# A third copy of the expert program: the second block of 32 tokens outside the loop

## What is computed

```python
def run_block(args):
    tok, e = args
    xb = xf[tok]
    hid = jax.nn.silu(xb @ w_gate[e]) * (xb @ w_up[e])
    return hid @ w_down[e]
...
y = jnp.zeros((n_tok, d), f32).at[buf_t].add(outs.reshape(cap, d).astype(f32) * buf_w[:, None])
```

## Time and profile before

| | us |
|---|---|
| median of 3 runs | 1020.96 |
| lowest and highest of them | 1017.95, 1021.09 |
| the profiled execution, its own time | 1017.99 |
| its span in the trace | 1016.3 |
| PE busy in the span | 813.8 |
| PEld busy | 658.0 |
| VectorE busy | 491.5 |
| ScalarE busy | 362.5 |
| GpSimd busy | 49.7 |
| read from HBM | 277.13 MB |

### The profile page before, as it was taken

How to read it: one execution, slowest core, us unless ns; L and a number is a source line. 1 busy time by engine, 2 the same in 40 slices (tenths; PEclk the granted TensorE clock), 3 DMA queues, 4 the chain that set the end, 5 groups by cost and what they waited for, 6 DMA issues and landing times.

```text
span 1016.3 us, 21184 instructions
## 1 busy us (share of the span) xinstructions
PE 813.8 (80%) x8057; PEld 658.0 (65%) x8058; DVE 491.5 (48%) x791; ACT 362.5 (36%) x505; POOL 49.7 (5%) x143
## 2 busy tenths in 40 slices
PE   5999789799999998879998787686655655767563
PEld 5999579699999998868988564353322332333231
DVE  3554788667878746555893633232312211232222
ACT  5432585364645544444873421111101011010102
POOL 4000100000000000110040000000000000000000
PEclk9999999799999999889999899898889887998887
DMA  7586222269898755053423956799999999999993
GB/s 262 185 285 232 84 83 84 92 257 352 292 314 292 262 200 170 17 166 115 133 85 127 425 221 249 309 423 429 427 425 425 429 425 424 428 427 426 425 429 137
DMA packets 88256, 278.71 MB, mean 274 GB/s; under 512 B 7279, under 2 KB 67098, under 8 KB 70810
## 3 DMA queue, kind: packets, MB, share of 16 engines
q1 hardware_dynamic: 87518, 276.84, 70.5%
q10 hardware_dynamic: 700, 1.36, 0.4%
HBM read 277.13 MB, written 1.05 MB: 274 GB/s over the span
## 4 chain that ended last, share of the span: by engine, by line
PE 58%; DMA 21%; DVE 9%; issue 5%; ACT 5%; PEld 1%; POOL 1%; SPq 0%; PEldq 0%; POOLq 0%; DVEq 0%; ACTq 0%
DMA Whi<-in_w_up 20%; PE bank L1785 10%; PE bank L380 9%; PE bank L381 9%; PE bank L382 9%; PE bank L1806 3%; PE acc L431 2%; PE bank L1515 1%; PE acc L1520 1%; PE acc L1515 1%; PE bank L1518 1%; PE acc L1518 1%; PE bank L1520 1%; DVE rms L437 1%; PE bank L1797 1%
## 5 line engine op out<-in xcount | busy, mean ns | idle before, releaser
L380 PE MATMUL bank<-R_r,Whi_r 128*128 128x256 f32 x800 | 233.3, 292 | 18.6 <-DVE R_r L2065 7.2
L381 PE MATMUL bank<-R_r,Whi_r 128*128 128x256 f32 x800 | 230.5, 288 | 0.0
L382 PE MATMUL bank<-R_r,Whi_r 128*128 128x256 f32 x720 | 207.1, 288 | 0.0
L380 PEld LDWEIGHTS bank<-R_r,Whi_r 128*128 128x128 f32 x800 | 157.6, 197 | 24.0 <-issue 18.3
L381 PEld LDWEIGHTS bank<-R_r,Whi_r 128*128 128x128 f32 x800 | 157.8, 197 | 0.1
L382 PEld LDWEIGHTS bank<-R_r,Whi_r 128*128 128x128 f32 x720 | 141.7, 197 | 0.0
L2518 DVE TENSOR_TENSOR V<-V,bank 64x256 f32<-64x256 f32 x34 | 14.4, 424 | 244.2 <-ACT V L1282 244.2
L1785 PE MATMUL bank<-Whi,S 128*32 128x256 f32 x832 | 65.0, 481 | 43.8 <-DMA Whi<-in_w_up 29.0
L1282 ACT ACTIVATE V<-bank 64x256 f32<-64x256 f32 x34 | 12.8, 376 | 213.7 <-PE bank L1785 213.7
L311 ACT ACTIVATE Whi_r<-Wlo 128x1024 fp32r<-128x1024 f32 x64 | 63.9, 1049 | 66.7 <-PE bank L382 66.3
L2010 DVE TENSOR_TENSOR Whi_r<-Wlo,Whi_r 128x2048 fp32r<-128x2048 f32 x33 | 75.6, 2289 | 25.0 <-ACT Whi_r L1083 12.2
(11 more groups left out here) (490 smaller groups left out, 1583.6 us busy)
## 6 DMA issues: line engine op xcount, KB each, us to landing
Wlo<-in_w_in SPq DMA_DIRECT2D x24, 1024.0 KB, 5.3
Wlo<-in_w_gate_up SPq DMA_DIRECT2D x22, 1024.0 KB, 5.1
Whi<-in_w_gate SPq DMA_DIRECT2D x10, 2048.0 KB, 26.0
Whi<-in_w_up SPq DMA_DIRECT2D x10, 2048.0 KB, 30.4
Whi<-in_w_down SPq DMA_DIRECT2D x10, 2048.0 KB, 32.2
projR<-in_w_up SPq DMA_DIRECT2D x9, 2048.0 KB, 37.0
Wlo<-in_w_gate SPq DMA_DIRECT2D x9, 2048.0 KB, 27.1
Wlo<-in_w_up SPq DMA_DIRECT2D x9, 2048.0 KB, 31.5
```

The source lines that it names most:

```text
L380: pe.matmul(o, w_hi[:, c], tile(x_hi, k), start=(k == 0), stop=False)
L381: pe.matmul(o, w_hi[:, c], tile(x_lo, k), start=False, stop=False)
L382: mm = pe.matmul(o, w_lo[:, c], tile(x_hi, k), start=False, stop=(k == KT - 1))
```

## The change

On GpSimd, ScalarE, TensorE and VectorE alike, the second window of an expert gets straight code of its own behind `If(windows > 1)`. The inner loop runs over w = 2 to 7, and stands behind a second test, `If(windows > 2)`. Each par holds three copies of the window program, nine in all. No operation, wait, transfer or buffer changes.

```diff
@@ gpsimd
                     gather(0)
                     with pool.If(windows > 1):
-                        with pool.Fori(1, NWIN) as w:
-                            with pool.If(windows > w):
-                                gather(w)
+                        gather(1)
+                        with pool.If(windows > 2):
+                            with pool.Fori(2, NWIN) as w:
+                                with pool.If(windows > w):
+                                    gather(w)
@@ scalar
                     window(before + 1)
                     with act.If(windows > 1):
-                        with act.Fori(1, NWIN) as w:
-                            with act.If(windows > w):
-                                window(before + w + 1)
+                        window(before + 2)
+                        with act.If(windows > 2):
+                            with act.Fori(2, NWIN) as w:
+                                with act.If(windows > w):
+                                    window(before + w + 1)
@@ tensor
                     window(None, before + 1)
                     with pe.If(windows > 1):
-                        with pe.Fori(1, NWIN) as w:
-                            with pe.If(windows > w):
-                                window(w, before + w + 1)
+                        window(1, before + 2)
+                        with pe.If(windows > 2):
+                            with pe.Fori(2, NWIN) as w:
+                                with pe.If(windows > w):
+                                    window(w, before + w + 1)
@@ vector
                     window(0, before + 1)
                     with dve.If(windows > 1):
-                        with dve.Fori(1, NWIN) as w:
-                            with dve.If(windows > w):
-                                window(w, before + w + 1)
+                        window(1, before + 2)
+                        with dve.If(windows > 2):
+                            with dve.Fori(2, NWIN) as w:
+                                with dve.If(windows > w):
+                                    window(w, before + w + 1)
```

## The result

The changed kernel is slower: 1184.37 us (median of 4; 1178.05 to 1185.3) against 1020.21 us (median of 4; 1017.95 to 1021.09), a ratio of 1.160 with a 95% interval of 1.1555 to 1.1645, or +164 us. The forecast was 1019.9 us, the range 1016 to 1046; of its cases the strong form of "code that no longer stays" came true, and above its own price.

The account below looks back on a forecast made before the run. The prediction took the weight stream as the bound, so of TensorE's 26 us only the filled dip counted: -1.15 + 0.1 for more code = -1.05 us, from 1020.96 to 1019.9 us, range 1016 to 1046.

Parts of the forecast that it names:

- strong form: Rival, 0.17: on TensorE each hop misses its code, a round takes 51 us, +66 us, about 1086 us.
- code that no longer stays: Rival, slower, 0.50: TensorE's loop body grows from 5.5 to 8.3 packets, no longer fits on chip, each round fetches again.
- What bounds the kernel: In the expert rounds the weight stream at about 427 GB/s is the bound, 14.7 us per expert, not an engine.
- Steps 1 and 2: TensorE after ranks 1, 5, 18 and 20: empty passes gone, 17.7 us; faster clock for the next experts, 8.4 us.
- Step 3: Second windows on TensorE gain 0; the weight stream's dip at 656 to 664 us is filled, -1.15 us.
- Step 4: Three more window copies in TensorE's program, 2.8 instruction packets to fetch: bounds 0 and +2.9 us, +0.1 taken.
- mild form: Rival, 0.33: only a round's last and first code on TensorE displace each other; +11.1 us, 1031 us.
- The hop's price: TensorE's jump over a copy to code not kept: 4.8 us under load, an estimated 2 us at idle.
- The hole: Rival, 0.05: weight stream's standstill at 636 to 640 us closes if rank 0's exit shortens; -4.4 us more, 1015.5 us.
- The exit: In the mild form, TensorE behind the last expert: three more jumps at 2 us, 1.3 us free, +4.7 us.

Follow-up runs that it names:

- e7: Changed kernel without the inner loop of buffers 1 and 2 on all four engines, seven copies: 1015.96 us, ratio 0.9981 against the kernel before.
- e5: Kernel before, plus a never-run third window copy in TensorE's program for buffer 0 only, seven copies: 1017.86 us.
- e6: Kernel before, plus never-run third window copies in TensorE's program for buffers 0 and 1, eight copies: 1111.81 us.
- e10: Changed kernel with every weight transfer from rank 3 on cut to an eighth, instructions and waits the same: 1075.62 us.
- e4: Kernel before, two copies kept, inner loop ending at the expert's own number of windows on all four engines: 1013.01 us, ratio 0.9956.
- e3: Kernel before, plus a never-run third window copy per buffer in TensorE's program, inside the outer loop: 1198.32 us.
- e9: Kernel before, plus 22 never-run combines (352 matmuls) in TensorE's program between the outer loop and the end: 1020.44 us.

## Why the prediction was wrong, step by step

- **What bounds the kernel: right.** The stream bound before, and where TensorE's 26 us were freed without growing past the store (e7) they brought 1.9 us (0.4 to 3.6).
- **Steps 1 and 2, gaps and clock: right in e7, undone in the changed kernel.** TensorE in order of time of the changed kernel, its ranks 1 and 2:

```profile
626.17 5.16 PE L1789 MATMUL bank<-Wlo,S 128*32 128x256 f32 x64 [4.69 <-issue]
...
643.28 0.63 PE L1789 MATMUL bank<-w_gate,S 128*32 128x256 f32 x4 [0.84 <-issue]
...
647.69 0.64 PE L1789 MATMUL bank<-projR,S 128*32 128x256 f32 x2 [3.79 <-issue]
```

  The gap after rank 1 is 0.84 us instead of 5.39, as forecast (0.67); but four matmuls later TensorE stands for 3.79 us, at what I read as the first packet not yet fetched. Rank 5's load is issued at 654.22, not at 647.4: from 654.88 before, nothing is won.
- **Step 3, second windows and the dip: right in e7**, -1.9 us measured for -1.05.
- **Step 4, more code: the step that failed.** I bounded it from what a packet costs once (0 to 2.9 us, +0.1 taken), that is, as if each extra packet were fetched one time. The question was how often. The runs show some ten packets in every round, 86 behind 664 us, and +164 us, where the sum had +0.1. The trace of before shows that 5.5 packets and headers stay, and the changed loop has 8.3 and headers. "As likely as not" was fair for the store's size, and the rival named the mechanism; but I gave the forecast 0.45 and the strong form 0.17, and ended the range at 1046, ahead of the strong form's own time. Seven copies fit and eight don't, by e5 and e6: the changed kernel, with nine, was two past the step. The Trainium skill, "Runtime: NRT & Kernel Launch", section "Instruction fetch mechanics", gives TensorE eight blocks of 16 KiB; read as a size of what a loop may hold, e5 and e6 agree to within a packet: 7 x 0.92 = 6.4 packets and headers stay, 7.4 and headers don't. By size alone eight copies could still fit into eight blocks; they don't only if the packet ahead, or a block that the body fills in part, counts too, and no run splits that. I had cited it as neither shown nor refuted, and should have let it shift the chances.
- **The mild form (0.33): wrong.** It let only the round's last and first code displace each other. The rows show ten packets in each round and a gap ahead of every expert.
- **The strong form: right in mechanism, 98 us short in size (1086 for 1184).** Three terms were small. The gaps of a round were put at 22 us and measure 30.5: the crossing inside the third expert (2.46 us) was not counted, and the round's end takes 14.73 us instead of 11.0. The windows were put at 29.1 us and take 61.15 - 30.5 = 30.65. So a round is 17 us over the stream, not 7, and eight rounds make 8 x 17 = 136 us. The third is the pace of before: its eight rounds, from rank 3's load at 618.40 to rank 27's at 955.78 us, took 337.4 us and not 8 x 44.1 = 352.8, which is 15.4 us more. In the changed kernel the same loads lie at 617.87 and 1115.44 us, 497.6 us apart, 8.4 us over 8 x 61.15: the round with rank 18's second window takes 68.80 us. Those with the second windows of ranks 5 and 20, at a round's end, take only 61.92 and 61.77, since the gap behind such a window is 8.60 and 8.48 us instead of 14 to 15. With 7.5 us behind the last of these loads that is 136 + 15.4 + 8.4 + 7.5 = 167 us, the difference of the two spans.
- **The hop's price (4.8 us under load, 2 us idle): a microsecond low.** In the rounds shown the gaps between experts are 6.47 and 6.81 us, and 3.62 and 3.97 us with a light stream; 0.67 of each is there anyway, so a hop is 5.8 to 6.1 and 3.0 to 3.3 us. The round's end was the expensive one. The sequencer's row for the loop's closing branch in the changed kernel (ns), and in e10:

```profile
L1826 PEldq COMPARE_BRANCH  x1: 7407/7407/7407, 847.4 to 847.4; - x1
```

```profile
L1829 PEldq COMPARE_BRANCH  x1: 4737/4737/4737, 750.0 to 750.0; - x1
```

- **The hole (0.05): wrong for this change, right as a mechanism.** It stayed open, since rank 0's exit kept its gap (4.69 us). e4 closed it and gained 4.5 us, where the rival said 5.5.
- **The exit: near.** The rival put its three jumps, less what is free, at +4.7 us; the gap ahead of the last combine grew by 3.8. In the changed kernel the gap ahead of the last expert is 8.76 us, and ahead of the last combine 6.05, where 2.23 stood:

```profile
1159.01 4.97 PE L1789 MATMUL bank<-Whi,S 128*32 128x256 f32 x64 [8.76 <-issue]
...
1173.87 1.23 PE L1768 MATMUL acc<-T_r 32*128 32x256 f32 x16 [6.05 <-issue]
```

## What to carry to other kernels

Before the body of a loop on TensorE grows, count its instructions, matmul and weight load each as one, and look at the instruction queue behind the first round: zero packets there says that the body fits, and by how much it may grow must be tried, with copies that never run if need be. When the body no longer fits, the cost isn't the extra code once but code in nearly each round, and waits that a transfer stream had caused before hide only part of it (here 122 of 290 us). To get rid of empty passes, bound the loop by the data (e4): it adds no code, and it closes the hole that the copy leaves. It measured -4.5 us (-6.5 to -2.5) where the copy without its size measured -1.9 (-3.6 to -0.4), each against the kernel before beside it; the two intervals overlap.

## What was new about the hardware

- On TensorE a loop with seven window copies (6.4 packets of 16 KB, and headers) runs without a fetch; with eight, 62 packets are fetched behind 664 us, and with nine 86, nine to eleven a round.
- Code inside the loop counts even when it is never executed (e3, +18%); code behind the loop doesn't (e9, 1020.44 us where the kernel before lay at 1015.78 to 1021.01).
- A missed jump between two experts leaves a gap of 5.8 to 7.5 us beside a stream of some 310 GB/s and 3.6 to 4.6 us beside a light one; the jump back to the loop's start takes 7.4 and 4.7 us. Even with the light stream the misses cost 181 us; the full stream adds 109, the smaller part.
- With eight copies the fetching paused for a whole round, twice (727 to 759 and 998 to 1027 us), each time behind a round whose last expert had two windows. By what rule packets are replaced stays open.
- Gaps and the granted clock add up: it stood at 0.73 to 0.74, between the 1.2 and 2.4 GHz levels, in 700 to 900 us, where TensorE was idle half the time, and the same matmuls took 29.8 us longer from rank 3 on.
